# Three groups of transposes moved in TensorE's list, at the end of the sparse-attention layer

## The reference

```
sc  = q @ kc.T * scale - slope * dist_c ; p_c = masked_softmax(sc)   ; o_cmp = p_c @ vc   # 15 compressed blocks
ss  = q @ k_sel.T * scale - slope * dist; p_s = masked_softmax(ss)   ; o_sel = p_s @ v_sel
sw  = q @ k_win.T * scale - slope * dist; p_w = masked_softmax(sw)   ; o_win = p_w @ v_win
o   = g0 * o_cmp + g1 * o_sel + g2 * o_win ;  y = o @ w_out
```

## Time and profile before

| | |
|---|---|
| median of 3 runs | 1284.05 us (1283.46 to 1284.75) |
| profiled execution | 1283.19 us |
| its span, first to last instruction | 1281.5 us |
| mean granted TensorE clock | 0.993 |
| instructions | 19572 |

### The profile page before, as it was taken

The page is one execution under the profiler, slowest core; times in us unless marked ns, Lnnn a source line. Parts: engine busy times, 40 slices in busy tenths (PEclk is TensorE's granted clock), DMA queues, the critical chain, the costliest instruction groups (busy, mean ns, idle before and its releaser), DMA issues.

```text
span 1281.5 us, 19572 instructions
## 1 busy us (share of the span) xinstructions
PE 1247.1 (97%) x7756; PEld 1110.4 (87%) x7756; DVE 887.6 (69%) x931; ACT 641.2 (50%) x825; POOL 172.2 (13%) x217
## 2 busy tenths in 40 slices
PE   3999999999999999989999999999999999999998
PEld 2899899888888899978988888888889998988887
DVE  6769666676666767987766667666667687766665
ACT  2445545554444456855544444444446676644442
POOL 8400100088200110000100001000001221200000
PEclk9999899999999999999999999999999999999999
DMA  9897495455556362324555554665554444456551
GB/s 364 267 315 270 160 328 179 149 194 184 186 191 196 117 220 66 128 71 131 182 183 194 195 183 147 229 197 187 180 191 160 148 153 151 151 192 196 196 196 66
DMA packets 167104, 236.88 MB, mean 185 GB/s; under 512 B 5172, under 2 KB 146624, under 8 KB 164992
## 3 DMA queue, kind: packets, MB, share of 16 engines
q1 hardware_dynamic: 165920, 234.57, 54.8%
q0 software_dynamic: 816, 0.89, 0.3%
q10 hardware_dynamic: 304, 0.53, 0.1%
HBM read 234.92 MB, written 1.05 MB: 184 GB/s over the span
## 4 chain that ended last, share of the span: by engine, by line
PE 86%; DVE 6%; DMA 4%; ACT 2%; POOL 1%; issue 1%; DVEq 0%; ACTq 0%; POOLq 0%
PE acc L2191 23%; PE acc L2193 12%; PE acc L2227 5%; PE acc L2228 5%; PE acc L2229 5%; PE acc L2209 4%; PE acc L2210 3%; PE acc L2211 3%; DVE wlo L1355 2%; DMA raw<-in_w_in_dram 2%; PE acc L2599 2%; PE acc L2245 2%; PE acc L2128 2%; DVE region L1362 1%; PE acc L2129 1%; PE acc L2130 1%
## 5 line engine op out<-in xcount | busy, mean ns | idle before, releaser
L1355 DVE TENSOR_TENSOR wlo<-raw,whi 128x2048 fp32r<-128x2048 f32 (+1 forms) x199 | 453.8, 2283 | 200.1 <-ACT whi L746 199.2
L746 ACT ACTIVATE whi<-raw 128x2048 fp32r<-128x2048 f32 (+1 forms) x199 | 378.1, 1904 | 183.5 <-PE acc L2229 113.1
L2191 PE MATMUL acc<-hT,whi 128*128 128x512 f32 x1280 | 320.2, 392 | 0.5 <-ACTq L827 0.5
L2191 PEld LDWEIGHTS acc<-hT,whi 128*128 128x128 f32 x1280 | 232.4, 189 | 43.9 <-issue 0.7
L2193 PEld LDWEIGHTS acc<-hT,wlo 128*128 128x128 f32 x1280 | 174.6, 190 | 12.5
L2193 PE MATMUL acc<-hT,wlo 128*128 128x256 f32 x1280 | 178.5, 282 | 0.0
L2227 PE MATMUL acc<-whi,sT_hi 128*128 128x512 f32 x320 | 125.0, 391 | 0.0
L2228 PE MATMUL acc<-wlo,sT_hi 128*128 128x512 f32 x320 | 125.0, 390 | 0.0
L2229 PE MATMUL acc<-whi,sT_lo 128*128 128x512 f32 x320 | 124.5, 389 | 0.0
L2209 PE MATMUL acc<-whi,hT 128*128 128x256 f32 x416 | 120.2, 289 | 1.1 <-DVE hT L1429 1.1
L2210 PE MATMUL acc<-wlo,hT 128*128 128x256 f32 x416 | 117.6, 283 | 0.0
(11 more groups left out here) (324 smaller groups left out, 1952.2 us busy)
## 6 DMA issues: line engine op xcount, KB each, us to landing
raw<-in_ffn_w_in_dram SPq DMA_DIRECT2D x88, 1024.0 KB, 5.1
raw<-in_ffn_w_out_dram SPq DMA_DIRECT2D x44, 1024.0 KB, 5.0
raw<-in_w_ada_dram SPq DMA_DIRECT2D x24, 1024.0 KB, 5.6
raw<-in_w_in_dram SPq DMA_DIRECT2D x24, 1024.0 KB, 6.0
raw<-in_diff_w_in_dram SPq DMA_DIRECT2D x12, 1024.0 KB, 5.2
raw<-in_nsa_w_in_dram SPq DMA_DIRECT2D x10, 1024.0 KB, 5.3
raw<-in_w_out_dram SPq DMA_DIRECT2D x8, 1024.0 KB, 5.0
raw<-in_nsa_cmp_w_dram SPq DMA_DIRECT2D x4, 1024.0 KB, 5.5
```

The costliest lines, as they stand in the source:

```text
L746: nc.scalar.activation(whi[:, w % SPL, 0:n], raw[:, r % RAW, 0:n], ACT.Copy).then_inc(hi_ready, 1)
L1355: nc.vector.tensor_tensor(wlo[:, w % SPL, 0:n], raw[:, r % RAW, 0:n], whi_f[:, w % SPL, 0:n], ALU.subtract).then_inc(raw_done, 1)
L2191: nc.tensor.matmul(o, hi[:, kt, cs], hT[:, :, kt, :], start=kt == 0, stop=False)
```

## The change

Only the order of calls in TensorE's list changes. The transposes of step 12 go from behind the value product of step 11 to a place in front of the scores of step 14; those of step 13 from behind to in front of the value product of step 12; those of step 15, with the value product of step 14 behind them, to a place in front of the scores of step 17. No instruction is added or removed, every wait stays with its instruction, and the lists of the other engines stay as they are.

```
             turn_q(3)
             nsa_turn(11)
             select_v()
+            nsa_turn(12)
             nsa_scores(14)
             nsa_values(11)
-            nsa_turn(12)
+            nsa_turn(13)
             nsa_values(12)
-            nsa_turn(13)
             nsa_scores(15)
             nsa_turn(14)
             nsa_values(13)
             nsa_scores(16)
+            nsa_turn(15)
+            nsa_values(14)
             nsa_scores(17)
-            nsa_values(14)
-            nsa_turn(15)
             nsa_turn_o(0)
             nsa_scores(18)
             nsa_turn_o(1)
```

## The result

The changed kernel takes 1292.56 us (median of 20 runs, 1286.87 to 1296.45) against 1284.84 us for the kernel before in the same comparison (20 runs, 1281.63 to 1292.64). The ratio is 1.0056, 95% interval [1.0043, 1.0070]: slower by 7.2 us, between 5.5 and 9.0. The forecast was slower by 3.75 us, 1287.8, with 1290.0 as the upper end; the direction holds, the time lies 2.6 us above the range.

What follows compares the result with a forecast made beforehand. TensorE was taken as busy for 97% of the span, with VectorE the bound in the edited stretch. Order 2.1 plus clock 1.65 gave 3.75 us, 1286.9 against the profiled 1283.19; 0.86 more for the median gave 1287.8, range 1285.6 to 1290.0.

Steps and rivals of the forecast that it cites:

- walk: Part-by-part timing of the moved transposes of steps 12, 13 and 15, with running totals +1.0, +1.7 and +2.1 us.
- What bounds the stretch: Steps 11 to 15: VectorE is the bound; its `combine(11)`, not ScalarE's copy of step 12, ends the 1.32 us gap.
- The order's cost, + 2.1 us: Waits in front of other work at the three moved transposes start step 15's value product at 575.45, not 573.35 us.
- The clock, + 1.65 us: Near step 15's transposes: TensorE falls to 1.2 GHz for 3.4 us as before, costing 0 to 1.7 us, taken as 1.65.
- what shifts it shifts the end: TensorE has no gap behind step 15's value product until the layer ends, so that product's delay is the kernel's.
- the mark of the sum: Start of step 15's value product, 573.35 us before, by which the prediction measured the change.
- The clock stays low longer or falls twice: Rival: longer low clock, or a second fall, for instance before step 13's transpose; another 1.5 us, +5.3, 1289.4; chance 0.17.
- The clock does not fall on the path: Rival: gap too short, or the fall comes where VectorE is the bound; +2.1 us, 1286.15; chance 0.22.
- absorbed the delay: Rival: slack on VectorE and a faster start of the projection leave under +1 us, about 1285; chance 0.08.
- starts before its old place: Sign of the not-slower rival (1282.9 us, chance 0.03): step 12's value product starts before 560.95 us.

Runs made afterwards that it cites:

- e10: Changed kernel with 16 extra 512-column products of no use in its waits and 3 more ahead of the edited place: 1287.0 us, ratio 1.0015.
- e8: The changed kernel once more with no edit, for a second profile: 1293.11 us.
- e2: Kernel before with 7 extra products of no use in its two waits of over 1 us: 1283.4 us, ratio 0.9996.
- e3: Kernel before with only step 15's transposes and step 14's value product moved in front of the scores of step 17: 1290.24 us, ratio 1.0054.
- e5: Changed kernel with 8 extra products of no use in front of step 15's transposes only: 1289.67 us, ratio 1.0023.
- e6: Kernel before with step 15's transposes moved in front of step 14's value product, scores of step 17 kept ahead of both: 1284.23 us, ratio 0.9999.

## Why the prediction was right in its walk and wrong in its size

*What bounds the stretch.* Right. In all profiles of the changed order in which the two big waits stand, they end with VectorE's mask (line 1750) and ScalarE's exp (1041), the releasers that the walk named, and the copy of step 12, which the profile of before named, is not among them.

*The order's cost, + 2.1 us.* Right. With the clock up the value product of step 12 starts 12.82 us into the stage in e10, and 12.71 in e8, where the clock falls only 0.4 us before and no product was added; the walk had 562.65 - 550.08 = 12.57. That of step 15 starts at 25.58; the walk had 575.45 - 550.08 = 25.37. The 2.1 is the distance from 23.27, which contains a fall of the clock, and e10 and e2 confirm both parts: 25.58 - 23.27 = 2.3, and 23.27 - 21.72 = 1.55 for the fall.

*The clock, + 1.65 us.* This step failed. The prediction put it as "I take it that the clock falls there too, for the 3.4 us that it did before". It does fall there, in both profiles of the changed kernel and in e3, but stays down for 13.7 us, four times as long. With it fails "what shifts it shifts the end": the start of the value product of step 15, the mark of the sum, does not carry the loss. From the mark to the end of the stage it is 30.4 to 30.5 us in every profile in which the clock is up there, of either order, and 34.1 to 34.5 us in the three with the long fall (e3, e8, changed). That is 3.7 to 4.1 us behind the mark, where the sum had nothing. Ahead of the mark the long fall costs about what the prediction gave the clock: from the value product of step 14 to that of step 15 it is 4.17 us in e10 and 6.00 in e8, 1.8 us more. The last part of the loss in e8 is 0.8 us, from the value product of step 14 starting at 22.18 in place of 21.41 us, with a fall of 3.4 us at the wait before step 13's transpose; the prediction had this fall as a rival only.

At 0.31 to 0.40 us each (e8 and e5 against the changed kernel), 13.7 us at the low clock cost 4.2 to 5.5. The sum for e8, + 3.9 for the order with the clock up, 17.1 x 0.36 = 6.2 for the low clock (0.36 from 62.29 - 56.07 = 6.22 over the 17.1), less the 1.5 that the kernel before pays, is 8.6: by construction the difference of the two stages, 62.29 - 53.66. In the prediction's terms, against its 2.1 + 1.65 = 3.75: 2.4 for the order (56.07 - 53.66), then 0.8, 1.8 and 3.6 for the clock. The same from the runs, without traces: the median mean clock of the changed kernel's 20 runs is 0.987 against 0.992 of the kernel before (81 runs), and twice 0.013 and 0.008 of the spans are 34 and 21 us at half speed. 13 us more at 0.36 is 4.7, with 3.9 for the order at the full clock 8.6, against 7.2 [5.5, 9.0] measured; the mean clocks are given to 0.001 only, which is 2.6 us of low time.

*Why it stays down.* This stays open. In the kernel before, nearly all of 12 transposes, and eight score instructions of 128 columns run in the 3.4 us of low clock (the last four transposes of the earlier trace rows start at 572.83, 0.1 us before it is back, so the prediction's "16 transposes" is four too many). In e6, too, it is back after 3.4 us, with the later ones of eight transposes, the value product of step 14 (eight instructions of 64 columns) and four transposes in them. So neither transposes nor a value product of 64 columns is enough to hold it down. In e3 and e8 the eight score instructions of 30 columns stand in these first 3.4 us as well, and the clock is not back. What follows then runs slower (the 16 instructions of 64 columns of step 15 last 3.51 us in place of 1.90), and the clock comes back 2.5 to 2.6 us after the first 512-column product of the output projection. That e3's place for step 15 brings the long fall and e6's does not is shown by one profile each and by 12 runs each whose ratios lie apart. Two things differ between them, the 0.9 us more of wait and the score instructions behind it in place of ahead of it, and they were not separated.

The Trainium skill, "TensorE: Matmul & The Clock Gate", Part 4, had been weighed for its rule that transposes don't count as busy for the clock. No run here decides it: in the kernel before, transposes take some two of the 3.4 us at the low clock, and it comes back all the same, but other products stand among them.

*The rivals.* "The clock stays low longer or falls twice" is what happened; it had a chance of 0.17 and + 5.3 us, since I gave it only 1.5 us more, again one fall of the size seen before. "The clock does not fall on the path" would have been 1286.15 and is nearest to e10, where the clock was held up through the stage; but there the added products also spare the 1.5 us that the kernel before pays. Nothing absorbed the delay, and value product 12 never starts before its old place.

*What the prediction could have seen.* It had one profile, which has one fall of 3.4 us in this stretch, and the three runs shown (1283.46 to 1284.75) had no long one among them. The lever was there: the same trace has a fall of 10.2 us, from 142.9 us on. I read the length of a fall off a single instance.

## What to carry to other kernels

Here the order of TensorE's list changed how long the clock was low as well as the waits: a wait put in front of small work cost more through the clock behind it than through itself, and the loss shows as more busy time on TensorE with the same instructions. Price such an edit for a longer fall than the one seen (here 13.7 us in place of 3.4, at 0.31 to 0.40 us each), look through the whole trace for the longest fall, and count the instructions behind the edit too. Where a wait can't be avoided, work with no use in it may pay: three products ahead and seven in the waits took 0.2% (0.07 to 0.35%) off this kernel.

## What the runs showed of the hardware

The clock fell without any wait on TensorE: from 550 to 554 us of the changed kernel TensorE was busy for 4.00 of 4.00 us (first stretch in the section on the result), and at 553.5 us the granted clock went to 1.2 GHz for 17.1 us. The kernel before has such a fall too: the one of 10.2 us begins at 142.9 us, in the middle of this row:

```profile
140.07 4.27 PE L2279 MATMUL acc<-ones,region 128*128 128x1 f32 x32
```

It then lasted over a wait of 2.09 us and 2.7 us of products of 256 columns.

The fall at 553.5 us lies ahead of every edit, and e8, with the same list, had none there: the rows of TensorE are alike up to that point of the stage. So the same instructions in the same order get different clocks in different executions; what decides it is not shown. The kernel before ranges from 1281.0 to 1294.5 us, and its time goes with the clock: over its 81 runs the span rises by 0.30 us for each us at half speed.
